# A diffusion step of two layers on one core: the second FFN product in another order of its token chunks

## What is computed

```python
def swiglu(h, w_in, w_out):
    g, u = jnp.split(h @ w_in, 2, axis=-1)
    return (jax.nn.silu(g) * u) @ w_out
...
    fp = swiglu(xp * (1.0 + sc2_p) + sh2_p, ffn_w_in[i], ffn_w_out[i])
    fs = swiglu(xs * (1.0 + sc2_s) + sh2_s, ffn_w_in[i], ffn_w_out[i])
    xp = layer_norm(ALPHA * xp + g2_p * fp, ln2_g[i], ln2_b[i])
    xs = layer_norm(ALPHA * xs + g2_s * fs, ln2_g[i], ln2_b[i])
```

## Time and profile before

| | us |
|---|---|
| median of 3 runs | 3561.7 (3560.54 to 3563.13) |
| the profiled execution, its own time | 3566.07 |
| its span, from first to last instruction | 3564.3 |
| PE busy | 3461.0 (97%) |
| DVE busy | 1514.7 (42%) |
| POOL busy | 1242.5 (35%) |
| ACT busy | 1038.9 (29%) |

### The profile page before, as it was taken

The page is one execution under the profiler, slowest core; times in us unless marked ns, Lnnn a source line. Parts: engine busy times, 40 slices in busy tenths (PEclk is TensorE's granted clock), DMA queues, the critical chain, the costliest instruction groups (busy, mean ns, idle before and its releaser), DMA issues. The chain is left out here.

```text
span 3564.3 us, 47143 instructions
## 1 busy us (share of the span) xinstructions
PE 3461.0 (97%) x19104; PEld 3017.3 (85%) x19104; DVE 1514.7 (42%) x2557; ACT 1038.9 (29%) x1558; POOL 1242.5 (35%) x819
## 2 busy tenths in 40 slices
PE   8999999989999999999999999999999999999997
PEld 8988887778888888888888778998888888888886
DVE  6856535656244444444441117887242111211116
ACT  5512111335311111111352316776252111111113
POOL 6411117436322222222451206665352222222223
PEclk9999999999999999999999999999999999999999
DMA  4533327542222222222163448775201111111111
GB/s 175 191 114 121 123 83 258 191 177 71 71 65 71 66 70 66 71 77 68 64 216 145 163 149 195 184 188 124 104 30 36 42 36 42 36 36 42 40 38 65
DMA packets 173814, 365.92 MB, mean 103 GB/s; under 512 B 16967, under 2 KB 98439, under 8 KB 171944
## 3 DMA queue, kind: packets, MB, share of 16 engines
q1 hardware_dynamic: 168168, 352.55, 31.0%
q10 hardware_dynamic: 5440, 10.49, 0.9%
HBM read 285.38 MB, written 77.59 MB: 102 GB/s over the span
## 5 line engine op out<-in xcount | busy, mean ns | idle before, releaser
L148 POOL TENSOR_TENSOR w_lo<-w_raw,w_hi 128x1024 fp32r<-128x1024 f32 x207 | 503.6, 2433 | 1414.7 <-ACT w_hi L142 1414.5
L156 PE MATMUL ps_r<-a_hi,w_hi 128*128 128x512 f32 (+1 forms) x2496 | 887.6, 356 | 2.6 <-POOL a_lo L2006 2.0
L156 PE MATMUL ps_r<-a_lo,w_hi 128*128 128x512 f32 (+1 forms) x2496 | 885.3, 355 | 0.0
L156 PE MATMUL ps_r<-a_hi,w_lo 128*128 128x512 f32 (+1 forms) x2496 | 884.2, 354 | 0.0
L156 PEld LDWEIGHTS ps_r<-a_hi,w_hi 128*128 128x128 f32 x2496 | 473.3, 190 | 73.2 <-POOL a_lo L2006 5.9
L156 PEld LDWEIGHTS ps_r<-a_lo,w_hi 128*128 128x128 f32 x2496 | 473.4, 190 | 65.7 <-issue 1.0
L156 PEld LDWEIGHTS ps_r<-a_hi,w_lo 128*128 128x128 f32 x2496 | 473.1, 190 | 65.8
L142 ACT ACTIVATE w_hi<-w_raw 128x1024 fp32r<-128x1024 f32 x207 | 217.4, 1050 | 727.9 <-PE ps_r L156 540.2
L2215 DVE TENSOR_TENSOR hid_l<-hid_l,ps_r 128x1280 f32<-128x1280 f32 x44 | 65.4, 1487 | 825.1 <-PE ps_r L156 825.1
L2235 DVE SCALAR_TENSOR_TENSOR x_t_l<-ps_r,mod,x_t_l 128x1024 f32<-128x1024 f32 (+1 forms) x288 | 241.3, 879 | 260.3 <-PE ps_r L156 260.3
L156 PE MATMUL ps_front<-x_split_f,w_hi 128*128 128x512 f32 (+1 forms) x1152 | 308.4, 356 | 0.0
(11 more groups left out here) (257 smaller groups left out, 6061.4 us busy)
## 6 DMA issues: line engine op xcount, KB each, us to landing
w_raw<-in_w_all SPq DMA_DIRECT2D x205, 512.0 KB, 3.5
ada_w_l<-in_ada_t SPq DMA_DIRECT2D x59, 512.0 KB, 3.5
v_hl<-v_d SPq DMA_DIRECT2D x128, 128.0 KB, 2.9
t_tail_f<-in_ada_t SPq DMA_DIRECT2D x24, 512.0 KB, 4.1
spec<-gout_f SPq DMA_DIRECT2D x80, 128.0 KB, 2.1
g_spec_c<-spec ACTq DMA_DIRECT2D x20, 512.0 KB, 5.0
v_d<-z_v_l SPq DMA_DIRECT2D x10, 1024.0 KB, 4.5
q_hl_l<-q_d SPq DMA_DIRECT2D x32, 320.0 KB, 7.3
```

The source lines that it names most:

```text
L148: pool.tensor_tensor(wl[:, s, 0:width], raw[:, s, 0:width], wh[:, s, 0:width].bitcast(F32), ALU.subtract).then_inc(w_split, 1)
L156: last = pe.matmul(out[:, c0:c1], w[:, c % 2, blk * 128:blk * 128 + 128], x[:, c0:c1], start=start and b == 0 and term == 0, stop=stop and ...
```

## The change

The order of the chunks becomes first 512, context, other 512 (`order2 = (0, 2, 1)`); the last chunk stays the same. The places are moved: with c the place in the order, `stat` at m = 3, `spread` at m = 5 of the second chunk and m = 4 of the third, `variance` at m = 2, `inverse` at m = 4 and m = 3, `root` at m = 4 and m = 3. The pieces of `normalise`, `modulate` and `low` for the first chunk stand at m = 5 and 7 of the second and m = 0 and 1 of the third, those for the second at m = 5 and 6 of the third. The QKV products that run over the statistics of the last chunk are cut differently. The low half of the last hidden tile is made for the new first chunk (now 512 columns) and then for the 768 others (before 256 and then 1024).

```diff
-                    products(pe, e0 + j, [(k, a_h[:, k, :], a_l[:, k, :], pg[j])], (CHUNKS[ORDER[ci]],),
+                    products(pe, e0 + j, [(k, a_h[:, k, :], a_l[:, k, :], pg[j])], (CHUNKS[(0, 2, 1)[ci]],),
...
-                order2 = ORDER
+                order2 = (0, 2, 1)
...
-                            if ci and m == 2:
+                            if ci and m == 3:
                                 stat(n2, ci - 1)
-                            if ci and m == 4:
+                            if ci and m == 6 - ci:
                                 spread(n2, ci - 1)
...
-                        qkv_first(pe, 0, 0)
+                        qkv_first(pe, 0, 0, range(4))
                         stat(n2, 2)
-                        qkv_first(pe, 1, 0)
+                        qkv_first(pe, 0, 0, range(4, KT))
                         means(n2, 2)
-                        qkv_first(pe, 0, 1, range(2))
+                        qkv_first(pe, 1, 0, range(2))
                         spread(n2, 2)
-                        qkv_first(pe, 0, 1, range(2, KT))
+                        qkv_first(pe, 1, 0, range(2, KT))
+                        qkv_first(pe, 0, 1)
                         qkv_first(pe, 1, 1)
...
+                    PLACES = {(1, 5): (0, 0), (1, 7): (0, 2), (2, 0): (0, 4), (2, 1): (0, 6), (2, 5): (1, 0), (2, 6): (1, 2)}
...
-                            if ci and m == 2:
+                            if ci and m == 4 - ci // 2:
                                 root(n2, ci - 1)
...
-                            if ci == 1 and m >= 4 or ci == 2 and m in (4, 5):
-                                end_part(ci - 1, range(2 * m - 8, 2 * m - 6))
+                            if (ci, m) in PLACES:
+                                c, k = PLACES[ci, m]
+                                end_part(c, range(k, k + 2))
...
-                                pool.tensor_tensor(hl[:, 0, k, 0:LS], sg[:, 0:LS], hh[:, 0, k, 0:LS].bitcast(F32),
+                                pool.tensor_tensor(hl[:, 0, k, c1:TOK], sg[:, c1:TOK], hh[:, 0, k, c1:TOK].bitcast(F32),
...
-                            if ci and m == 1:
+                            if ci and m == 2:
                                 variance(n2, ci - 1)
-                            if ci and m == 2:
+                            if ci and m == 5 - ci:
                                 inverse(n2, ci - 1)
-                            if ci == 1 and m >= 4 or ci == 2 and m in (4, 5):
-                                normalise(n2, ci - 1, 2 * m - 8)
+                            if (ci, m) in PLACES:
+                                normalise(n2, *PLACES[ci, m])
```

More of the change, by code:

```diff
@@ L1496, in qkv_pe @@
                         pe.wait_ge(n2.lo, 16 + k + 1)
-                        last = products(pe, e0 + j, [(k, a_h[:, k, :], a_l[:, k, :], pg[j])], (CHUNKS[ORDER[2]],),
+                        last = products(pe, e0 + j, [(k, a_h[:, k, :], a_l[:, k, :], pg[j])], (CHUNKS[1],),
                                         k == 0, k == KT - 1)
@@ L2055, in _ @@
                     rounds(step_in, step_out)
+                    PLACES = {(1, 5): (0, 0), (1, 7): (0, 2), (2, 0): (0, 4), (2, 1): (0, 6), (2, 5): (1, 0)}
                     for ci in range(3):
@@ L2059, in _ @@
                             add_x(n2, m, ci)
-                            if not last_layer and (ci == 1 and m >= 4 or ci == 2 and m == 4):
-                                low(n2, ci - 1, range(2 * m - 8, 2 * m - 6))
+                            if not last_layer and (ci, m) in PLACES:
+                                c, k = PLACES[ci, m]
+                                low(n2, c, range(k, k + 2))
                             if not last_layer and ci == 2 and m == 3:
```

## The result

The changed kernel took 3570.2 us in the median of 11 runs (3564.9 to 3573.0), the kernel before 3563.1 in as many beside it. The ratio is 1.0019, with an interval of 1.0010 to 1.0028. So the change costs 5 to 7 us by the ratios. The first median lies above the forecast of 3563.2 and 1.2 us above its range of 3555 to 3569; the second, 3567.5, lies inside the range. The profiled execution took 3569.27 us, its span is 3567.5.

What follows compares the result with a forecast made beforehand. PE, busy 97% of the span, was taken to bound the kernel, so only waits, half clock and tail could change. Layer 0 +4.3 and layer 1 -2.8 us made +1.5: median from 3561.7 to 3563.2 us, range 3555 to 3569.

Steps and rivals of the forecast that it cites:

- Part 1: First four pairs, both layers: PE's 2.57 us wait for L2219 shrinks to 0.6 us; the wait for L2043 goes.
- Part 2: First spread, both layers: the diagonal comes late, a new PE wait of 2.3 us in each.
- Part 3: Second statistics, layer 0: DVE and POOL collide, 5.9 us wait plus 1.7 us of low clock; 0.6 us wait in layer 1.
- The sum of layer 0: Layer 0's waits and low clock: 6.8 us before, 11.1 us after, so +4.3 us.
- The base of the sum: Layer 0 before the change: half clock costing 1.7 and 1.5 us, counted as loss that goes.
- Part 4: QKV head: last sums covered, the 0.42 us wait and 1.5 us of low clock go, no `low` makes a wait.
- Part 5 and layer 1: Layer 1's tail: eight normalise instructions narrow to 256 columns, -2.1 us; with -0.7 from its waits, layer 1 gains 2.8 us.
- (b): Rival: clock falls behind each new wait, two low periods behind the long one, one more POOL instruction; 3569.6 us, chance 0.12.
- (a): Rival: in layer 0's second statistics the locks miss each other, costing 0.6 to 1 us; 3556.6 us, chance 0.26.
- (c): Rival: everything hidden, first spread too, as the table loads while ACT waits for the variance; 3551.8 us, chance 0.10.

Runs made afterwards that it cites:

- x_after: The changed kernel, unaltered, timed and profiled a second time beside the kernel before: ratio 1.0013 (1.0004 to 1.0022).
- x_before: The kernel before, unaltered, profiled a second time: ratio 1.0005 (0.9996 to 1.0014).
- l1_only: New order at the end of layer 1 alone, layer 0 as in the kernel before: ratio to that kernel 0.9997 (0.9988 to 1.0006).
- weight: Changed kernel with layer 0's two QKV weight halves moved behind the root: ratio to the kernel before 0.9999 (0.9990 to 1.0008).
- psumvar: Changed kernel with the variance's two multiplications reading one operand from PSUM: ratio to the kernel before 1.0003 (0.9994 to 1.0012).
- second: Changed kernel with both QKV weight halves behind the root and the variance reading PSUM: ratio to the kernel before 0.9999 (0.9990 to 1.0008).
- l0_only: New order at the end of layer 0 with its QKV head, layer 1 as in the kernel before: ratio to that kernel 1.0017 (1.0008 to 1.0026).
- early: Changed kernel with the root's table loaded ahead of the end part and the root right behind the variance: ratio to the kernel before 1.0000 (0.9991 to 1.0009).

## Why the prediction was wrong, by its own steps

- **Part 1, right.** The wait for the weight's low half was predicted at 0.6 us and is 0.6; that for L2043 is gone in both layers.
- **Part 2, the wait right, its clock wrong.** 2.3 us were predicted, 2.2 and 2.1 measured. The sum gave it no clock fall in either layer, by the one row where the same length left the clock alone. Of the six profiles with this wait in layer 0 five show the fall, of the six with it in layer 1 three, and each costs about 1.7 us. This is the larger part of what failed.
- **Part 3, the waits right, their clock too small in the profile after.** 5.9 us were predicted, 5.4 and 6.3 measured, with the chain nearly as laid out; in layer 1 0.6 us were predicted and 0.4 measured. The 0.4 us in front of the second statistics are not there in the kernel after (0.2 in x_after). The clock behind the long wait was taken at 1.7 us. All four profiles with this wait have 6.8 us at half clock. In that of the kernel after 6.0 us of them lie behind the wait and cost 3.0; in x_after PE came sooner, waited 6.3 us, and only 3.3 us lie behind it, which cost 1.7, as predicted.
- **The sum of layer 0.** In the profile after the waits are 0.6 + 2.2 + 5.4 + 0.4 = 8.6 us, where the sum had 9.4, and the clock behind them costs 1.7 + 3.0 = 4.7, where it had 1.7. That is 13.3 for "11.1": +2.2, and A grew by 6.5 and not 4.3. **The term that failed is the clock behind the new waits:** nothing behind the first ones and one low period behind the long one. x_after, without a fall behind the first waits, has A at +5.1 and B at -2.9 against before, which is near the forecast of +4.3 and -2.8.
- **The base of the sum, nearly harmless by luck.** A cost of 3.2 us for the half clock before was booked as a loss that the change takes back. x_before and l1_only have no fall in layer 0 and the same A (94.7 and 94.8). So it was almost no loss: in its place stand waits of 2.3 us. And the row without a fall in layer 1 is not a property of the place: x_before, the same kernel, has the fall in layer 1 and none in layer 0.
- **Part 4, nearly right.** No new wait shows up at the QKV products in the profile after, and the low clock there is gone. But PE's first half tile did not cover the last sums: the third statistics waited 0.4 us for L2098.
- **Part 5 and layer 1, the size right only where the clock stays up.** -2.8 us were predicted. B is 85.9 to 86.0 (-2.8) in x_after, weight and psumvar, but 88.6, 87.5 and 88.2 in after, l1_only and second, where the fall comes. In the kernel after, the tail saved 1.0 us and not 2.1: from the end of the last `add_square` to COPY it is 3550.58 - 3546.86 = 3.7 us, against 3547.39 - 3542.69 = 4.7 before and 3550.74 - 3548.17 = 2.6 in x_after. In the first the clock was already at half when PE's last sums began (3546.5 and 3547.0 us), so that they came behind the normalising and not beside it; in x_after it fell at 3550.0 us, when they were nearly done. With the 1.7 us behind the first wait this makes the 2.7 us between the two values of B. COPY in the timeline of after:

```profile
3550.58 0.17 DVE L2108 COPY st_in_l<-ps_r 128x16 f32<-128x16 f32 x1 [1.08 <-PE ps_r L1699]
```

and of x_after, where it waits for nothing:

```profile
3550.74 0.16 DVE L2108 COPY st_in_l<-ps_r 128x16 f32<-128x16 f32 x1
```

Over the profiles with each order, A is 101.1 on the mean (after, x_after, l0_only) against 94.8 (before, x_before, l1_only), +6.3. B is 87.0 over the six with the changed end of layer 1 and its first wait, against 88.7, -1.7. Together +4.6 us, or 1.0013; the two measurements say 1.0013 and 1.0019. What is above 4.6 us in the first is within its interval, and no stretch outside A and B shows it.

Of the rivals, (b) names what happened in the profiles of after and l0_only: falls behind the new waits, and two low periods behind the long one. That its 3569.6 us stands beside the measured 3570.2 is partly luck. It counted 1.3 us for one more POOL instruction, which did not come (the wait was 5.4 us and not 7.2), it started from 3561.7 where the kernel before took 3563.1 this time, and x_after has no fall behind a first wait. It had a chance of 0.12, because I let one row without a fall outweigh the row with one. Against (a) stands the trace: the locks met nearly as laid out, in each of the two profiles. Of (c), its mechanism (the table loaded while ACT waits) did not come by itself; put in by hand, in early, it took the first wait away.

## What to carry to other kernels

A wait that a reordering opens on TensorE costs its length and may cost half-clock time behind it (here waits of 2.1 us and more); book both, and treat the fall as likely unless several executions show none. What counts of a fall is the part behind the wait: the part inside it costs nothing. A fall that the old kernel has is worth only what remains once the waits it stands for come back, so look at a second profile before it is counted as a gain. And a better order is not finished when its products are: here it lost 0.13 to 0.19% by itself and won 0.23 to 0.31% once the root's table, the variance's operands and two weight halves were out of the new critical chain's way.

## What the runs showed of the hardware

- Waits of PE of 2.1 to 2.8 us were followed by half clock or not, whatever their length. In the old order the 2.6 us wait for the weight's low half had it in one of four profiles in layer 0 and in two of four in layer 1; the first new wait had it in five of six in layer 0 and three of six in layer 1, second waits of 2.2 to 2.8 us in none of three. The waits of 5.4 and 6.3 us had it in four of four, twice as long (6.8 us), and there it began 0.7 to 4.0 us before the wait ended. What decides among the short ones was not tried. Among the first QKV products 3.4 us of half clock stood in all four profiles of the new order with the early root and in none of the six without it; why is open too.
- DVE's small instructions with all operands in SBUF (128x4) take 0.17 us alone and up to 1.3 beside a 128x512 instruction of POOL, also the one with a single operand, L2114 above (1.21, beside the sum L2002). The same instruction took 0.17 us in psumvar, where it stood between two of POOL's subtractions, and 1.34 in second. With one operand in PSUM they took 0.16 beside POOL's subtraction.
- The root began 0.02 us behind the end of its table load before. Loaded ahead of the end part, the table costs nothing that A or B shows.
